# Strassen's seven products for part of the FFN's up projection, with weight sums on GpSimd and closing sums on DVE

## What is computed

```python
h = rms_norm(x, g_mlp_pre)
f = jnp.square(jax.nn.relu(h @ w_up)) @ w_down     # w_up 1024 x 4096, w_down 4096 x 1024
return x + rms_norm(f, g_mlp_post)
```

## Time and profile before

| | |
|---|---|
| median of the runs | 2458.11 us |
| span of the profiled execution | 2455.7 us |
| TensorE busy in the span | 99% |
| DVE, ACT, GpSimd busy | 54%, 38%, 12% |
| matmuls | 12348 |

### The profile page before, as it was taken

The page is one execution under the profiler, slowest core; times in us unless marked ns, Lnnn a source line. Parts: engine busy times, 40 slices in busy tenths (PEclk is TensorE's granted clock), DMA queues, the critical chain, the costliest instruction groups (busy, mean ns, idle before and its releaser), DMA issues.

```text
span 2455.7 us, 31484 instructions
## 1 busy us (share of the span) xinstructions
PE 2437.2 (99%) x12348; PEld 1991.3 (81%) x12348; DVE 1321.1 (54%) x1761; ACT 941.3 (38%) x1359; POOL 292.5 (12%) x237
## 2 busy tenths in 40 slices
PE   9999999999999999999999999999999999999998
PEld 7877988889876888888988888877778788888886
DVE  7764732434966563243543437769995386343322
ACT  4345532333445453232432235532335554322321
POOL 1231000001122100000111123400000121111101
PEclk9999999999999999999999999999999999999999
DMA  4312222222231222222222235643342143222222
GB/s 165 142 44 69 86 103 103 86 103 103 78 129 35 103 86 100 89 103 94 79 103 102 93 103 174 206 164 116 142 149 83 63 152 129 100 88 102 78 98 81
DMA packets 46253, 259.64 MB, mean 106 GB/s; under 512 B 5504, under 2 KB 6016, under 8 KB 23232
## 3 DMA queue, kind: packets, MB, share of 16 engines
q1 hardware_dynamic: 43712, 248.42, 29.0%
q0 software_dynamic: 640, 5.51, 0.6%
q10 hardware_dynamic: 1792, 4.20, 0.5%
HBM read 240.27 MB, written 16.78 MB: 105 GB/s over the span
## 4 chain that ended last, share of the span: by engine, by line
PE 91%; DVE 6%; ACT 2%; issue 1%; DMA 0%; DVEq 0%; SPq 0%; ACTq 0%
PE gemm L451 74%; DVE out_sb L1599 2%; PE gemm L733 1%; DVE w_lo L401 1%; PE gemm L744 1%; PE gemm L735 1%; PE gemm L698 1%; PE gemm L699 1%; PE gemm L696 1%; PE turned L1135 1%; PE mixed L1147 1%; PE score L1124 1%; PE gemm L626 1%; PE gemm L627 1%; PE gemm L635 1%
## 5 line engine op out<-in xcount | busy, mean ns | idle before, releaser
L401 DVE TENSOR_TENSOR w_lo<-w_raw,w_hi 128x2048 fp32r<-128x2048 f32 (+2 forms) x207 | 439.2, 2122 | 480.7 <-ACT w_hi L393 480.3
L451 PE MATMUL gemm<-h_hi,w_hi 128*128 128x512 f32 x1744 | 691.2, 396 | 2.6 <-DVE w_lo L401 2.2
L451 PE MATMUL gemm<-h_hi,w_lo 128*128 128x512 f32 x1744 | 679.9, 390 | 0.0
L451 PE MATMUL gemm<-h_lo,w_hi 128*128 128x512 f32 x1744 | 679.2, 389 | 0.0
L393 ACT ACTIVATE w_hi<-w_raw 128x2048 fp32r<-128x2048 f32 (+3 forms) x217 | 381.9, 1760 | 345.5 <-PE gemm L451 302.8
L451 PEld LDWEIGHTS gemm<-h_hi,w_hi 128*128 128x128 f32 x1744 | 327.7, 188 | 81.8 <-issue 9.1
L451 PEld LDWEIGHTS gemm<-h_hi,w_lo 128*128 128x128 f32 x1744 | 327.3, 188 | 69.6
L451 PEld LDWEIGHTS gemm<-h_lo,w_hi 128*128 128x128 f32 x1744 | 327.8, 188 | 65.7 <-issue 1.0
L451 PE MATMUL gemm<-f_hi,w_hi 128*128 128x512 f32 x448 | 174.3, 389 | 0.0
L451 PE MATMUL gemm<-f_lo,w_hi 128*128 128x512 f32 x448 | 174.3, 389 | 0.0
L451 PE MATMUL gemm<-f_hi,w_lo 128*128 128x512 f32 x448 | 174.3, 389 | 0.0
(11 more groups left out here) (462 smaller groups left out, 3816.0 us busy)
## 6 DMA issues: line engine op xcount, KB each, us to landing
w_raw<-in_w SPq DMA_DIRECT2D x171, 1024.0 KB, 4.8
w_raw<-in_w SPq DMA_DIRECT2D x16, 768.0 KB, 4.2
w_raw<-in_w SPq DMA_DIRECT2D x16, 640.0 KB, 3.8
w_raw<-in_w SPq DMA_DIRECT2D x18, 512.0 KB, 3.6
trig_kept<-made SPq DMA_DIRECT2D x16, 512.0 KB, 5.7
trig<-trig_kept SPq DMA_DIRECT2D x16, 512.0 KB, 6.2
bias_t<-in_att_bias SPq DMA_DIRECT2D x2, 1536.0 KB, 8.1
decay_t<-in_c_decay SPq DMA_DIRECT2D x2, 1536.0 KB, 8.1
```

The costliest lines, as they stand in the source:

```text
L401: dve.tensor_tensor(flat(w_lo, b), flat(w_raw, b), flat(w_hi, b).bitcast(F32), ALU.subtract).then_inc(S["w_rest"], 1)
L451: mm = pe.matmul(dst, lhs, rhs, start=b.first and k == 0 and j == 0, stop=b.last and k == b.kt - 1 and j == 2)
```

## The change

d_ff is now taken in four quarters, each with 4 up pieces and then 4 down pieces (1024 rows each). The first quarter's up pieces stay as they were. In the other three quarters an up piece (1024 x 256, seen as 2 x 2 blocks of 512 x 128; the tokens are two halves of 256) is made from seven half-size products in Strassen's scheme (Winograd's form), each 4 k-tiles x 3 matmuls with 256 moving columns. GpSimd makes four sums of the weight blocks in float32 (`seven_sums`), ACT rounds the seven weight terms and DVE makes their rests, one term at a time (`term_round`, `term_rest`), during the seven products of the piece before; each term has one buffer. ACT copies the first product out of PSUM and DVE adds the others to it in seven sums of 256 columns (`two_products` to `first_late`). For this h itself is needed with its scale applied (`h_whole`), and sums of its blocks, made once a layer during the first quarter's down pieces: DVE scales and rests, GpSimd subtracts (`tokens_summed`), ACT rounds into `h_hi` and `t_hi`. The loops are written out. Down tiles of the first quarter are copied, those of the other three added by DVE. One down piece instead of two runs in token halves at a layer's end. On DVE each step of a piece is: a closing sum, then the rest of the next piece's term of the same number, then in steps 0 and 1 the rest of an f tile of the piece before.

```diff
-    for half in range(2):
-        for j in range(8):
-            out.append(Piece(0, half * 2048 + j * WCOLS, WCOLS, KD, "feat", "w_up"))
+    for part in range(D_FF // KB):
         for j in range(4):
-            for kb in range(2):
-                out.append(Piece(half * 2048 + kb * KB, j * WCOLS, WCOLS, KD, "feat", "w_down",
-                                 group=("down", half, j)))
+            out.append(Piece(0, part * KB + j * WCOLS, WCOLS, KD, "seven" if part else "feat", "w_up"))
+        for j in range(4):
+            out.append(Piece(part * KB, j * WCOLS, WCOLS, KD, "feat", "w_down"))
...
+        def term_of(buf, b, q):
+            c = slice(4 * P * (q % 4), 4 * P * (q % 4) + 4 * P)
+            return buf[:, b.split if q < 4 else 1 - b.split, c]
...
+        def term_source(b, q):
+            return (quarter_of(b, 0), quarter_of(b, 3), w_sums[:, 1, :], w_sums[:, 0, :], quarter_of(b, 1),
+                    quarter_of(b, 2), w_sums[:, 2, :])[q]
...
+        def seven_sums(pool, b):
+            a11, a12, a22, a21 = [quarter_of(b, q) for q in range(4)]
+            one, three, four = [w_sums[:, q, :] for q in range(3)]
+            pool.wait_ge(w_in_s[b.slot], ONCE.loads(b.n))
+            if b.count:
+                pool.wait_ge(S["term_lo"], 6 * b.count - 2)
+            pool.tensor_tensor(one, a21, a22, ALU.add).then_inc(S["w_summed"], 1)
+            pool.tensor_tensor(three, a11, a21, ALU.subtract).then_inc(S["w_summed"], 1)
+            pool.wait_ge(S["w_summed"], summed_at(b, 2))
+            pool.tensor_tensor(a21, one, a11, ALU.subtract).then_inc(S["w_summed"], 1)
+            pool.wait_ge(S["w_summed"], summed_at(b, 3))
+            if b.count and not b.opens:
+                pool.wait_ge(S["w_rest"], b.n)
+            pool.tensor_tensor(four, a12, a21, ALU.subtract).then_inc(S["w_summed"], 1)
...
+        def term_round(act, b, q):
+            if b.opens:
+                act.wait_ge(S["units"], plan[b.n - (2 if q < 4 else 1)].u1)
+            elif q < 6:
+                act.wait_ge(S["term_read"], 6 * b.count - 5 + q)
+            else:
+                act.wait_ge(S["units"], b.u0)
+            if q in (0, 4, 5):
+                act.wait_ge(w_in_s[b.slot], ONCE.loads(b.n))
+            else:
+                act.wait_ge(S["w_summed"], summed_at(b, {1: 3, 2: 2, 3: 1, 6: 4}[q]))
+            act.activation(term_of(w_hi, b, q), term_source(b, q),
+                           ACT.Copy).then_inc(S["term_hi"] if q < 6 else S["w_rounded"], 1)
...
+        def term_rest(dve, b, q):
+            if q < 6:
+                dve.wait_ge(S["term_hi"], 6 * b.count + q + 1)
+            else:
+                dve.wait_ge(S["w_rounded"], b.n + 1)
+            dve.tensor_tensor(term_of(w_lo, b, q), term_source(b, q), term_of(w_hi, b, q).bitcast(F32),
+                              ALU.subtract).then_inc(S["term_lo"] if q < 6 else S["w_rest"], 1)
...
+        def quarter_round(act, b, q):
+            last = closed_by(b)
+            act.wait_ge(S["term_read"], 6 * last.count + q + 1)
+            act.wait_ge(w_in_s[b.slot], ONCE.loads(b.n))
+            act.activation(term_of(w_hi, b, q), quarter_of(b, q),
+                           ACT.Copy).then_inc(S["more_hi"] if q < 3 else S["w_rounded"], 1)
...
+        def seven(pe, b):
+            y, w, z, x = [bank[q][:, 0:HALF] for q in b.banks]
+            direct, sums = (h_hi, h_lo), (t_hi, t_lo)
+            order = ((y, direct, 0, 0), (w, sums, 1, 1), (z, sums, 0, 1), (x, sums, 0, 0), (y, direct, 1, 0),
+                     (z, sums, 1, 0), (x, direct, 1, 1))
+            for q, (dst, (hi, lo), kh, e) in enumerate(order):
+                if q < 6:
+                    pe.wait_ge(S["term_lo"], 6 * b.count + q + 1)
+                else:
+                    pe.wait_ge(S["w_rest"], b.n + 1)
+                if q == 4:
+                    pe.wait_ge(S["first_out"], b.count + 1)
+                elif q > 4:
+                    pe.wait_ge(S["seven_out"], 7 * b.count + (2 if q == 5 else 4))
+                elif b.opens:
+                    if b.need[q]:
+                        pe.wait_ge(S["g_free"], b.need[q])
+                elif q != 1:
+                    pe.wait_ge(*((S["seven_out"], 7 * b.count - 2), None, (S["seven_out"], 7 * b.count - 1), (S["g_free"], b.t0))[q])
+                wh, wl = term_of(w_hi, b, q), term_of(w_lo, b, q)
+                for k in range(4):
+                    c = slice(P * k, P * k + P)
+                    h, r = hi[:, 4 * kh + k, TOKENS[e]], lo[:, 4 * kh + k, TOKENS[e]]
+                    pe.matmul(dst, wh[:, c], h, start=k == 0, stop=False)
+                    pe.matmul(dst, wh[:, c], r, start=False, stop=False)
+                    mm = pe.matmul(dst, wl[:, c], h, start=False, stop=k == 3)
+                mm.then_inc(S["term_read"] if q < 6 else S["units"], 1)
...
+        def two_products(dve, b):
+            dve.wait_ge(S["term_read"], 6 * b.count + 2)
+            dve.wait_ge(S["first_out"], b.count + 1)
+            dve.tensor_tensor(two_sum[:], out_tile(b, 1, 0), bank[b.banks[1]][:, 0:HALF],
+                              ALU.add).then_inc(S["seven_out"], 1)
+        def three_products(dve, b):
+            dve.wait_ge(S["term_read"], 6 * b.count + 3)
+            dve.wait_ge(S["seven_out"], 7 * b.count + 1)
+            dve.tensor_tensor(three_sum[:], two_sum[:], bank[b.banks[2]][:, 0:HALF],
+                              ALU.add).then_inc(S["seven_out"], 1)
+        def last_late(dve, b):
+            dve.wait_ge(S["term_read"], 6 * b.count + 4)
+            dve.wait_ge(S["seven_out"], 7 * b.count + 2)
+            dve.tensor_tensor(out_tile(b, 0, 1), three_sum[:], bank[b.banks[3]][:, 0:HALF],
+                              ALU.add).then_inc(S["seven_out"], 1)
+        def other_three(dve, b):
+            dve.tensor_tensor(two_sum[:], two_sum[:], bank[b.banks[3]][:, 0:HALF],
+                              ALU.add).then_inc(S["seven_out"], 1)
+        def first_early(dve, b):
+            dve.wait_ge(S["term_read"], 6 * b.count + 5)
+            dve.tensor_tensor(out_tile(b, 1, 0), out_tile(b, 1, 0), bank[b.banks[0]][:, 0:HALF],
+                              ALU.add).then_inc(S["seven_out"], 1)
+        def last_early(dve, b):
+            dve.wait_ge(S["term_read"], 6 * b.count + 6)
+            dve.tensor_tensor(out_tile(b, 0, 0), three_sum[:], bank[b.banks[2]][:, 0:HALF],
+                              ALU.add).then_inc(S["seven_out"], 1)
+        def first_late(dve, b):
+            dve.wait_ge(S["units"], b.u1)
+            dve.wait_ge(S["seven_out"], 7 * b.count + 5)
+            dve.wait_ge(S["g_free"], b.t0)
+            dve.tensor_tensor(out_tile(b, 1, 1), two_sum[:], bank[b.banks[3]][:, 0:HALF],
+                              ALU.add).then_inc(S["g_free"], 1)
...
-            for half in range(2):
-                first = plan1[UP[half]]
...
-            last_in_halves(pe, plan1[DOWN[1] + 6:DOWN[1] + 8], f_hi, f_lo, 2 * lay + 1, 6)
+            first = plan1[UP[0]]
+            opening_in_halves(pe, plan1[first.i:first.i + 2], 2 * lay, out_sb)
+            for b in plan1[first.i + 2:first.i + 4]:
+                product(pe, b, h_hi, h_lo, each=second_total(pe, 2 * lay, out_sb) if b.i == first.i + 2 else None)
+            for part in range(PARTS):
+                if part:
+                    if part == 1:
+                        pe.wait_ge(S["whole"], cnt("whole", KD + 4))
+                    for b in plan1[UP[part]:UP[part] + 4]:
+                        seven(pe, b)
+                    pe.wait_ge(S["seven_out"], 7 * b.count + 6)
+                for j, b in enumerate(plan1[DOWN[part]:DOWN[part] + 4]):
+                    if part < PARTS - 1 or j < 3:
+                        product(pe, b, f_hi, f_lo,
+                                tile_ready=None if j else (S["f_ready"], cnt("f_ready", KD * part)))
+            last_in_halves(pe, [b], f_hi, f_lo, 2 * lay + 1, 6)
...
+            b11, b12, b21, b22 = [h_whole[:, 4 * kh:4 * kh + 4, TOKENS[e]] for kh in range(2) for e in range(2)]
+            pool.wait_ge(S["whole"], cnt("whole", KD + 2))
+            tokens_summed(b11, b12, b11, ALU.subtract, 0)
+            tokens_summed(b12, b22, b12, ALU.subtract, 1)
+            tokens_summed(b22, b22, b11, ALU.subtract, 2)
+            tokens_summed(b21, b21, b22, ALU.subtract, 3)
+            for part in range(1, PARTS):
+                for b in plan1[UP[part]:UP[part] + 4]:
+                    seven_sums(pool, b)
...
+            def direct_round():
+                act.wait_ge(S["units"], plan1[UP[0] + 3].u1)
+                act.wait_ge(S["whole"], cnt("whole", 4))
+                act.activation(h_hi[:, 0:4, TOKENS[0]], h_whole[:, 0:4, TOKENS[0]],
+                               ACT.Copy).then_inc(S["more_hi"], 1)
+                act.wait_ge(S["whole"], cnt("whole", KD))
+                act.activation(h_hi[:, 4:KD, :], h_whole[:, 4:KD, :], ACT.Copy).then_inc(S["more_hi"], 1)
```

(80 more changed lines are left out.)

343 lines of the change are left out of this document (198 added, 145 removed).

## The result

The changed kernel takes 2464.9 us (median of eight runs, 2462.8 to 2468.0) against 2458.0 for the kernel before in the same comparison (2457.4 to 2458.3): ratio 1.0029, 95% interval 1.0021 to 1.0038. It is slower by 6.9 us where 2.9 us less were forecast.

A forecast was written before the change was run, and what follows sets the result against it. TensorE, busy 99% of the span, was taken to bound the kernel; matmul savings less DVE stalls gave -1.6, layer ends -1.3, so -2.9 on 2458.1: 2455.2 us. The forecast's range was 2448 to 2463, eight in ten 2443 to 2471.

The forecast's parts named there:

- 24 pieces on TensorE: FFN up pieces: 84 narrow matmuls (10.08 us) replace 48 wide ones (10.88), 12 pieces in each of 2 layers, -19.2 us.
- waits at `three_products`: TensorE waits for DVE in runs of four pieces: stalls of 0.7 and 1.8 us, 1.3 more in a layer's first run.
- two layer ends: Last down group: one piece instead of two in token halves, 0.64 us less a layer, -1.3 in all.
- granted clock: FFN stage: TensorE read as busy at full clock; the sum held no term for a change of clock.
- DVE's own piece of 8.5 us: Middle piece of a run: DVE's rests, squaring and closing sums take 8.5 us in TensorE's 10.08.
- 0.9 a sum: Price to DVE of each GpSimd weight sum in a run: 0.76 to 1.10 us, taken as 0.85 to 0.9.
- the restart: After a wait for DVE: matmul starts 0.05 after DVE's end, the next 0.34 instead of 0.227 later, 0.15 us in all.
- Rival 2: Middle pieces: DVE becomes the bound, GpSimd holding it 1.27 us a sum, cycle 13.6; +18 us, 2476; chance 0.32.
- that estimate of 2464: Skill's shared read port taken literally: 1.27 us a GpSimd sum instead of 1.10, 9 us more, 2464.
- rival 3: Up pieces: weight loads of 0.19 us bind at 84 a piece, 16 us a piece, +122 us; with unknown, chance 0.01.
- the part-0 down phase: First quarter's down pieces (43.5 us) hide h and token work; terms 0 to 3 rested 1.7 us before TensorE wants them.
- Rival 1: Middle pieces: GpSimd's conflict is hidden and TensorE binds, all 19.2 + 1.3 kept, 2437.6; with what lies between, chance 0.15.

The follow-up runs named there:

- e12: Changed kernel with early layer-end squares, weight sums of each run's second to fourth piece on DVE, f rests and two weight sums reordered on DVE: 2437.05 us.
- e1: Changed kernel with ACT squaring output tiles 2 and 3 right after tiles 0 and 1 at a layer's end: 2458.15 us.
- e13: Pair to e12: same early squares and places of the f rests, but every weight sum on GpSimd as in the changed kernel: 2450.22 us.
- e3: Changed kernel with GpSimd's weight sums written to buffers that no term reads, terms taken from raw blocks: 2464.56 us.
- e2: Changed kernel without GpSimd's four weight sums per piece, terms taken from raw blocks of the same size: 2445.97 us.
- e4: Changed kernel with weight sums of each run's second to fourth piece made by DVE, the first piece's still by GpSimd: 2451.68 us.
- e7: Changed kernel with DVE's two f rests moved from steps 0 and 1 to steps 3 and 4, sums still on GpSimd: 2461.36 us.
- e9: Edits of e1 and e2 together on the changed kernel, no weight sums and early squares at the layer's end: 2438.22 us.

## Why the prediction was wrong

The measured 2464.9 lies above the forecast's range of 2448 to 2463. Between the profiled spans, the forecast's -2.9 became +8.2:

| term | forecast | measured | how |
|---|---|---|---|
| 24 pieces on TensorE | -19.2 | -19.2 | runs of 40.31 in e12 |
| waits at `three_products` | +17.6 | +19.7 | the six runs, 263.1 less 1.5 of clock, against 241.9 in e12: 17.0 of idle time, the rest restarts |
| two layer ends | -1.3 | +4.3 | -0.64 each; waits of 2.89 and 2.54, restarts of 0.09 |
| granted clock | 0 | +3.0 | two falls of 1.5 |
| sum | -2.9 | +7.8 | span: +8.2; where the other 0.4 lies is not shown |

**The step that failed** is "The last down group ran two pieces in token halves (narrow) and now one does: 96 x 0.120 - 10.88 = 0.64 us less a layer, -1.3 in all." It counted matmuls and looked at no one who waits beside them. The rows were there: the earlier trace rows lie in that group, and its half sum waits for a chain through ACT, GpSimd and DVE that the kernel before had laid out over pairs of pieces. Halving the time between the pairs (10.9 us for 21.8) took the cover, and the sum said nothing of it, though this edit touches a reduction across three engines. It cost 5.4 us of waiting; e1 gives the whole price, clock included: 6.75 of the 9.8 us by which the forecast was off. With the layer's end put right the kernel takes 2458.15, 3.0 above the forecast and inside its range; restarts and clock, which the forecast had too small or not at all, go the same way.

**The waits at `three_products`** were in the right place, number and order: 1.78 and 1.74 in a first run, 0.76 (0.69 to 0.76) and 1.74 in the others, none in pieces 0 and 3, with the sum 17.0 against 17.6. DVE's own piece of 8.5 us and 0.9 a sum give 12.1; measured 12.04. What was mis-sized is the restart: 0.15 from the earlier trace rows, once a run, measured 0.24 at each wait (460.49 to 462.51 between starts, then 0.20, less two spacings of 0.12, is 1.98 lost for 1.74 of idle time). Rival 2 didn't come: the cycle is under its 12.3, and the second and third run of a layer take 43.25 us, not 43.5 + 2.8. The measured time lies in the band that the prediction gave to rival 2 (2463 to 2480), but another cause brought it there, so that band holds it by luck.

The Trainium skill, SBUF — State Buffer, section Who interferes with whom, has a DVE instruction with two SBUF inputs contend with a GpSimd instruction that reads SBUF, through an exclusive lock. The traces agree that only instructions with two SBUF inputs are held (closing sums stay at 0.41), but the price was 0.90 a sum and not the 1.27 that the prediction worked out from it; that estimate of 2464 is close to the result by chance, for the waits are 17.0 us where it would have had about 27. The Trainium skill, Perfetto Trace Analysis, section Optimizing Scalar/DVE Operations, warns that work moved between these two engines might not help; e13 against e12 agrees, with 13 us.

**The granted clock** was not in the sum at all. The earlier trace rows show 1.00 in a stage without waits, and the forecast put waits of 1.8 us into it without asking what they do to the clock. Falls differ from execution to execution: of 23 waits of 1.7 to 1.8 us in the traces of the changed kernel, e1 and e3, 2 were followed by one; of ten layer ends of 2.5 to 2.9 us (changed kernel, e2, e3, e4, e7) 7 had one, in two cases from before the wait's end; of the shorter waits in the runs none. They fit the spread: 5.2 us over eight runs of the changed kernel, with a mean granted clock of 0.998 at 2462.8 and 0.996 at 2468.0, against 0.65 over five of e12 and 0.8 before. The Trainium skill, TensorE: Matmul & The Clock Gate, section HAM oscillation — how this bites in real kernels, tells of the clock falling when bursts of matmuls alternate with waits; here that was the exception after 1.7 us and the rule after 2.5.

**What held**: the spacing of 0.120; weight loads that don't bind (rival 3); the part-0 down phase (terms 0 to 3 rested by 341.6, TensorE there at 342.94, 1.3 us of slack where 1.7 were worked out); GpSimd's sums of 1.29 to 1.75; no wait at a load or at `g_free`. Rival 1 became true only by other edits, in e9 and e12.

What stays open: why e12 is 1.2 us below e9, which has less work on DVE. Both have runs of 40.3 us, and up to the end of the second layer's FFN e12 is only 0.3 ahead (last down piece begun at 1172.31 and 1172.64); the rest arises in the third block, where no edit lies. How a wait's length and place decide on the clock was only counted, not tried.

## What to carry to other kernels

Before work goes from DVE to GpSimd, price what the GpSimd instruction takes from DVE against what DVE needs for it itself: here 0.90 against 0.60, so the offload made the late engine later, and making the sums on DVE in the right order, with the layer's end put right, won 20.8 us over the kernel before. When a stage is made finer, look at every chain that was hidden behind the coarser one, reductions for a norm above all, and count what its engines still have to do when the last piece begins. A short wait of TensorE costs more than its length: a restart, and sometimes a stretch at half clock.

## What the hardware showed that was not expected

- A wait of TensorE at `three_products` costs 0.24 us beyond its idle time, one at a layer's end 0.09. With 9 of 33 waits of 1.7 to 2.9 us came a stretch at a granted clock of 0.50, mostly 3.4 us long (6.8 once, in e4); one of 3.4 cost 1.5 us. Where the next wait is for another engine, that loss can be given back: in e1 the second wait of the first run shrank from 1.74 to 0.21 us after such a stretch, and the run took 44.26 us, in the second layer without a fall 44.28.
- A GpSimd instruction holds DVE by up to 1.10 us but by 0.90 on average here, as DVE instructions that read PSUM run beside it (454.11 in the timeline above); and it holds DVE just as much when nobody uses its result.
